# Attention scores of a hybrid decoder layer: from separate bias and maximum passes to one fused VectorE operation per head

## The chip, the cores and the metric

The kernel runs on one core of a Trainium2 chip. The metric is the device time of one execution in microseconds (us). The engines are named as in the profile: PE is TensorE (matmuls; PEld its weight loads), DVE is VectorE, ACT is ScalarE, POOL is GpSimd, SP is SyncE, which mostly issues transfers.

## What is computed

One decoder layer on 512 tokens of width 1024. A modulated norm and one projection feed two causal attention branches; their outputs are projected, gated, summed and normed; then comes a mixture of 32 experts, each token going to 4. Only the scores of the two branches are touched. A: 8 heads of width 64, a window of 128, one learned sink per head. B: 4 heads with two maps each, full causal. Both add a bias that depends on the distance alone, from one table with 32 buckets.

```python
# A (per head): qb holds q / 8
sc = where(valid, qb @ kb.T + bias, -inf)
m = maximum(max(sc, -1), sink)
p = exp(sc - m) / (sum(exp(sc - m)) + exp(sink - m))
# B (per head and map m): distances of 128 and more share one bucket
sc = where(dist >= 0, qb[m] @ k[m].T + bias, -inf)
p[m] = softmax(sc);   a = p[0] - lambda * p[1]
```

## The kernel before

Every engine has its own program, and semaphores tie them together. The stages follow one another: conditioning and norm, the input projection (w_in is streamed in halves, split into high and low parts), attention, the merge (output projection, norms, router, dispatch) and the experts, whose weights are streamed through SBUF.

In the attention stage the work is cut into 24 units: for each of four tiles of 128 queries (n = 0 to 3), two A units (one per group g, four heads in one unit) and four B units (one per head, two maps in one unit). An A unit has 4 rows of scores of 256 keys per query (128 in tile 0). A B unit has 2 rows of (n + 1) x 128 keys; the last 256 of them are "near" and get the table of biases, those before them are "far" and get one value per head.

A unit goes through the engines so. PE makes the scores in PSUM (`scores`, line 401; two pairs of banks in turn). VectorE (`before`, line 486) scales them by QK_SCALE = 1/8, adds the bias and writes them to SBUF: line 496 for an A unit, line 510 for the near part of a B unit, line 514 for the far part (tiles 2 and 3 only); each of these counts up `s_ready`. Then it reduces the maximum of each row (line 499 or 517) and negates it (line 501, with the sink, and line 504 for A; line 519 for B). ScalarE takes the exponentials with their sums (line 593). VectorE (`after`, line 521) divides (lines 529 to 533) or combines the two maps (lines 536 to 541). PE transposes the result (lines 430, 434), ScalarE copies that to SBUF (line 609), PE multiplies by the values (lines 451, 459). At the end of a tile a norm runs over B's outputs: squares on ScalarE (line 621), `sub_norm_begun` and `sub_norm` on VectorE (line 557 writes `on`), a power on POOL, four transposes on PE (line 467).

The order of the work is written out by hand: each engine walks over the units in a loop, VectorE with `after(i + 1)`, then `before(i + 3)`; ScalarE with the copy of i, the exponentials of i + 2, the outputs of i - 1; PE with the scores of i + 3, the transposes of i, the values of i - 1. PE's scores of unit i wait until the scores of unit i - 2 have been read out of PSUM (`s_ready`, line 405). The values of the first B unit of a tile wait for the norm of the tile before (line 457). Between VectorE's units 2 and 3 stand three operations (lines 565 to 569); line 565 needs `grow3`, whose load POOL issues behind the last columns of the input projection.

The bias tables are made long before: a matmul of the bucket table with a one-hot matrix gives vectors of 384 biases by distance, VectorE copies them to `rv` (line 1785), POOL stores them to HBM and reads them back shifted by one per partition as `toep` (128 queries x 12 heads x 256 keys). `farb` is the bias of the last bucket, and `sinkb` the sinks, for each partition. Masked places hold -1e30.

Of the kernel before, what the change touches and what calls it, by code (L numbers as in the profile page):

```python
# [14 lines left out]
F32 = mybir.dt.float32  # L15
# [8 lines left out]
P = 128  # L24
# [6 lines left out]
H_B = 4  # L31
# [65 lines left out]
def program(nc, ctx, x, c, rel_bias_table, w_ada, b_ada, g_mix_pre, g_mix_post, g_ffn_pre, g_ffn_post, w_in, w_out,  # L97
# [122 lines left out]
    nhalf = small("nhalf", [P, H_B], F32)  # L220
    cact = small("cact", [P, KC], F32)
    sinkb = small("sinkb", [P, H_A], F32)
    nsink = small("nsink", [P, H_A], F32)
    farb = small("farb", [P, H_B], F32)
    subg = small("subg", [P, 1], F32)
    subgs = small("subgs", [P, 1], F32)
    nlam0 = small("nlam0", [P, 1], F32)
# [13 lines left out]
    lprod = at("lprod", [P, 2, DH], F32, 158 * KB)  # L241

    st = at("st", [P, IN_FLIGHT, 8, 4], F32, 35 * KB)
    NMX, MX, DSK, ESK, SUM, DEN, FAC = range(7)
    sn = at("sn", [P, 3, H_B], F32, 35 * KB + 512)
    bsum = at("bsum", [P, 2, H_B], F32, 35 * KB + 576)
    beps = at("beps", [P, H_B], F32, 35 * KB + 608)
# [40 lines left out]
    def sem(name):  # L288
# [19 lines left out]
    s_ps, s_ready, mx_step, exp_ready, den_step, p_ready, t_ps, pt_ready, o_ps, o_ready = map(  # L308
        sem, ("s_ps", "s_ready", "mx_step", "exp_ready", "den_step", "p_ready", "t_ps", "pt_ready", "o_ps",
              "o_ready"))  # L310
    osq_ready, sn_ready, on_ready, ot_ps, ot_ready = map(
        sem, ("osq_ready", "sn_ready", "on_ready", "ot_ps", "ot_ready"))

# [45 lines left out]
    def total(count, i):  # L359
        return sum(count(u) for u in UNITS[:i + 1])  # L360

    def n_scores(u):
        return 2 if u[0] == "B" and u[1] >= 2 else 1

    def n_max(u):
        return 3 if u[0] == "A" else 2

    def n_exp(u):
        return 5 if u[0] == "A" else 2
# [30 lines left out]
    def attention_pe(pe):  # L400
        def scores(i):
            kind, n, g = UNITS[i]
            w = 2 * (i % 2)
            if i >= 2:
                pe.wait_ge(s_ready, total(n_scores, i - 2))
            if kind == "A":
                k0, k1 = keys(UNITS[i])
                for place in range(4):
                    a, b = place // 2, place % 2
                    lo = (place % 2) * 2 * P + (P if n == 0 else 0)  # L410
                    ins = nc.tensor.matmul(ps[:, w + a, lo:lo + (k1 - k0) * P],
                                           qk[64 * a:64 * a + 64, 2 * g + b, n * P:(n + 1) * P],
                                           ka2[64 * a:64 * a + 64, g, k0 * P:k1 * P], start=True, stop=True)
            else:
                for m in range(2):
                    ins = nc.tensor.matmul(ps[:, w + m, 0:(n + 1) * P], qk[64 * m:64 * m + 64, 4 + g, n * P:(n + 1) * P],
                                           qk[64 * m:64 * m + 64, 8 + g, 0:(n + 1) * P], start=True, stop=True)
            ins.then_inc(s_ps, 1)
# [64 lines left out]
    def attention_dve(dve):  # L483
        dve.wait_ge(toep_in, 16 * 5)

        def before(i):
# [6 lines left out]
            src, dst = scores_ps(i), scores_sb(i)  # L493
            if kind == "A":
                lo = P if n == 0 else 0
                nc.vector.scalar_tensor_tensor(dst, src, QK_SCALE, toep[:, 4 * g:4 * g + 4, lo:2 * P], ALU.mult,
                                               ALU.add).then_inc(s_ready, 1)
                dve.wait_ge(s_ready, total(n_scores, i))
                nc.vector.tensor_reduce(st[:, w, MX, :], dst, AX_X, ALU.max).then_inc(mx_step, 1)
                dve.wait_ge(mx_step, total(n_max, i) - 2)  # L500
                nc.vector.scalar_tensor_tensor(st[:, w, NMX, :], st[:, w, MX, :], -1.0, nsink[:, 4 * g:4 * g + 4],
                                               ALU.mult, ALU.min).then_inc(mx_step, 1)
                dve.wait_ge(mx_step, total(n_max, i) - 1)
                nc.vector.tensor_tensor(st[:, w, DSK, :], st[:, w, NMX, :], sinkb[:, 4 * g:4 * g + 4],
                                        ALU.add).then_inc(mx_step, 1)
                return
            near = max(n - 1, 0) * P
            width = (n + 1) * P - near
            tile = toep[:, H_A + g:H_A + g + 1, 2 * P - width:2 * P].to_broadcast([P, 2, width])
            nc.vector.scalar_tensor_tensor(dst[:, :, near:near + width], src[:, :, near:near + width], QK_SCALE, tile,  # L510
                                           ALU.mult, ALU.add).then_inc(s_ready, 1)
            if near:

                nc.vector.tensor_scalar(dst[:, :, 0:near], src[:, :, 0:near], QK_SCALE, farb[:, g:g + 1], ALU.mult,
                                        ALU.add).then_inc(s_ready, 1)
            dve.wait_ge(s_ready, total(n_scores, i))
            nc.vector.tensor_reduce(st[:, w, MX, 0:2], dst, AX_X, ALU.max).then_inc(mx_step, 1)  # L517
            dve.wait_ge(mx_step, total(n_max, i) - 1)
            nc.vector.tensor_scalar(st[:, w, NMX, 0:2], st[:, w, MX, 0:2], -1.0, None, ALU.mult).then_inc(mx_step, 1)

        def after(i):
# [1175 lines left out]
    def _(dve):  # L1697
# [84 lines left out]
        for b in range(2):  # L1782
            n = (H_A, H_B)[b]
            dve.wait_ge(rv_ps, b + 1)
            nc.vector.tensor_copy(rv[0:n, b, :], ps[0:n, 6 + b, 0:REL]).then_inc(rv_ready, 1)
        dve.wait_ge(small_in, 16 * N_SMALL)
        nc.vector.tensor_tensor(lprod[:], lp[:, 0::2, :], lp[:, 1::2, :], ALU.mult).then_inc(lam_step, 1)
        dve.wait_ge(lam_step, 1)
        nc.vector.tensor_reduce(lsum[:], lprod[:], AX_X, ALU.add).then_inc(lam_step, 1)
        nc.vector.tensor_scalar(subgs[:], subg[:], 1.0 - LAM_INIT, None, ALU.mult).then_inc(lam_step, 1)  # L1790
        nc.vector.tensor_scalar(nsink[:], sinkb[:], -1.0, None, ALU.mult).then_inc(lam_step, 1)
        dve.wait_ge(bada_in, 16)

        def unit(u, last=False):
# [130 lines left out]
```

## Time and profile before

| | us |
|---|---|
| median of 3 runs | 1743.36 (1741.38 to 1743.51) |
| profiled execution | 1744.51 |
| its span | 1742.2 |
| granted TensorE clock, mean over the span | 0.964 |
| attention stage, VectorE's first to last operation | 244.25 to 334.18 |
| first matmul of the merge that is on the chain of waits | 335.34 |

The profile comes from one execution. Times of instructions are counted from the start of the span; "busy" is the time in which an engine executes an instruction. The granted clock is a share of TensorE's full 2.4 GHz, so that 0.5 is 1.2 GHz. Two instructions of one engine can overlap in the timeline, since one starts while its forerunner writes out its last results.

### The profile page before, as it was taken

Reading aid. Unit: us, or ns where it says so; the run is one execution under the profiler, and the core shown is the slowest. Engines: PE = TensorE matmul, PEld = TensorE weight load, DVE = VectorE, ACT = ScalarE, POOL = GpSimd, SP = SyncE. Lnnn points to the kernel's source line nnn. Section 1 sums busy time; section 2 is a strip of 40 time slices with the busy share of each in tenths; the row PEclk is TensorE's granted clock in tenths of the full one; section 3 lists DMA queues with packets and bytes.
Section 4 is the critical chain, followed back from the end, with each engine's and each line's share of the span. In section 5 each row is a group of like instructions: output and inputs, shape, how many; then the busy total and the mean of one; then the engine's idle time right before and its main releaser. Section 6 shows DMA issues by size and latency. Waiting matters only on the chain.

```text
span 1742.2 us, 19602 instructions
## 1 busy us (share of the span) xinstructions
PE 1650.7 (95%) x7482; PEld 1294.0 (74%) x7482; DVE 1372.9 (79%) x1017; ACT 1098.0 (63%) x903; POOL 200.1 (11%) x156
## 2 busy tenths in 40 slices
PE   8999988787699999999999999999999999999994
PEld 3888865443478888888888888888888888888882
DVE  5564459545589898889988898989888998889894
ACT  3323236612467777777777777777777777777772
POOL 2200000202200100011000100010001100021112
PEclk9999998897699999999999999999999999999997
DMA  9865530113699999999999999999999999999964
GB/s 340 249 236 193 169 118 1 52 73 105 245 406 399 375 368 387 390 380 354 387 380 384 359 375 389 389 383 366 379 378 390 358 390 389 380 357 371 383 238 158
DMA packets 156725, 540.93 MB, mean 310 GB/s; under 512 B 13980, under 2 KB 15112, under 8 KB 156515
## 3 DMA queue, kind: packets, MB, share of 16 engines
q1 hardware_dynamic: 140880, 500.20, 75.5%
q0 software_dynamic: 13648, 35.26, 8.4%
q10 hardware_dynamic: 2100, 4.21, 0.7%
q8 instruction: 57, 0.93, 0.2%
q14 instruction: 40, 0.33, 0.0%
HBM read 522.94 MB, written 29.66 MB: 317 GB/s over the span
## 4 chain that ended last, share of the span: by engine, by line
PE 80%; issue 8%; DVE 5%; DMA 4%; ACT 1%; POOL 1%; POOLq 0%; SPq 0%; ACTq 0%; DVEq 0%
PE ps L1113 65%; PE ps L661 4%; PE ps L1087 4%; PE ps L1103 2%; PE ps L1622 1%; PE ps L1624 1%; PE ps L1623 1%; DMA raw<-in_w_ada 1%; DMA oh<-const_buckets 1%; PE ps L681 1%; DMA grow<-in_g_ffn_post 0%; DVE st L517 0%; DMA expert_sums<-yb,icur 0%; DMA xb<-h_ffn,stab 0%; DVE acc L1721 0%
## 5 line engine op out<-in xcount | busy, mean ns | idle before, releaser
L1231 DVE TENSOR_TENSOR wl<-rawm,wh 128x2048 fp32r<-128x2048 f32 x420 | 946.7, 2286 | 147.7 <-ACT wh L1160 143.2
L1160 ACT ACTIVATE wh<-rawm 128x2048 fp32r<-128x2048 f32 x420 | 802.0, 1919 | 260.8 <-PE ps L1113 260.8
L1113 PE MATMUL ps<-wh,xh 128*128 128x512 f32 x1120 | 360.3, 403 | 3.5 <-DVE xl L1244 3.5
L1113 PE MATMUL ps<-wl,xh 128*128 128x512 f32 x1120 | 346.8, 391 | 0.0
L1113 PE MATMUL ps<-wh,xl 128*128 128x512 f32 x1120 | 346.3, 390 | 0.0
L1113 PEld LDWEIGHTS ps<-wh,xh 128*128 128x128 f32 x1120 | 211.3, 189 | 53.2 <-DVE xl L1244 4.9
L1113 PEld LDWEIGHTS ps<-wl,xh 128*128 128x128 f32 x1120 | 211.1, 189 | 44.9
L1113 PEld LDWEIGHTS ps<-wh,xl 128*128 128x128 f32 x1120 | 211.4, 189 | 44.5
L1113 PE MATMUL ps<-wh,ah 128*128 128x512 f32 x560 | 179.4, 401 | 2.5 <-DVE al L1248 2.5
L1113 PE MATMUL ps<-wl,ah 128*128 128x512 f32 x560 | 174.1, 392 | 0.0
L1113 PE MATMUL ps<-wh,al 128*128 128x512 f32 x560 | 173.1, 390 | 0.0
L1316 POOL DMA_INDIRECT expert_sums<-yb,stab x32 | 50.9, 1589 | 1009.0 <-ACT yb L1194 752.1
L1113 PEld LDWEIGHTS ps<-wh,al 128*128 128x128 f32 x560 | 105.6, 189 | 23.1
L1113 PEld LDWEIGHTS ps<-wl,ah 128*128 128x128 f32 x560 | 105.4, 188 | 22.7
L1113 PEld LDWEIGHTS ps<-wh,ah 128*128 128x128 f32 x560 | 100.3, 189 | 19.6 <-issue 3.0
L1758 DVE TENSOR_TENSOR wlf<-raw,whf 128x2048 fp32r<-128x2048 f32 (+1 forms) x18 | 39.1, 2173 | 70.1 <-ACT whf L1483 70.1
L1483 ACT ACTIVATE whf<-raw 128x2048 fp32r<-128x2048 f32 (+1 forms) x18 | 32.7, 1818 | 67.7 <-PE ps L1624 61.3
L1622 PE MATMUL ps<-whf,hh 128*128 128x512 f32 (+1 forms) x192 | 71.3, 372 | 0.0
L1305 POOL DMA_INDIRECT xb<-h_ffn,stab x32 | 65.7, 2053 | 47.7 <-PE ps L1087 36.2
L1624 PE MATMUL ps<-whf,hl 128*128 128x512 f32 (+1 forms) x192 | 71.0, 370 | 0.0
L1623 PE MATMUL ps<-wlf,hh 128*128 128x512 f32 (+1 forms) x192 | 71.0, 370 | 0.0
L1186 ACT ACTIVATE ah<-ps 128x1024 fp32r<-128x1024 f32 x35 | 35.9, 1026 | 55.3 <-PE ps L1113 55.3
(256 smaller groups left out, 1588.2 us busy)
## 6 DMA issues: line engine op xcount, KB each, us to landing
rawm<-in_w_gate_up SPq DMA_DIRECT2D x280, 1024.0 KB, 9.8
rawm<-in_w_down SPq DMA_DIRECT2D x140, 1024.0 KB, 7.9
raw<-in_w_ada SPq DMA_DIRECT2D x20, 1024.0 KB, 5.9
raw<-in_w_in SPq DMA_DIRECT2D x16, 1024.0 KB, 5.6
rawx<-in_w_ada SPq DMA_DIRECT2D x4, 1024.0 KB, 15.7
wo<-in_w_out SPq DMA_DIRECT2D x2, 2048.0 KB, 12.6
bias_vectors_repeated<-bias_vectors POOLq DMA_DIRECT2D x1, 2304.0 KB, 15.2
xs<-in_x ACTq DMA_DIRECT2D x1, 2048.0 KB, 12.8
```

Source lines behind the costliest of these rows:

```text
L661: ins = nc.tensor.matmul(ps[:, 2 * b + half, :], src[:, k, t * P:(t + 1) * P], wo[:, 4 * b + k, half * UN:(half + 1) * UN], start=(k == 0) ...
L1087: ins = nc.tensor.transpose(TURNED[:, k // 4, (k % 4) * P:(k % 4 + 1) * P], src[:, k * P:(k + 1) * P], ident[:])
L1113: ins = nc.tensor.matmul(banks[:, n, :], left[:, kk, :], right[:, k, n * UN:(n + 1) * UN], start=begins and kk == 0 and i == 0, stop=kk == ...
L1160: nc.scalar.activation(flat(wh[v % SPL][:]), flat(rawm[v][:]), ACT.Copy).then_inc(wh_done, 1)
L1186: nc.scalar.activation(flat(ah[:]), flat(TURNED), ACT.Copy).then_inc(ah_done, 1)
L1231: nc.vector.tensor_tensor(flat(wl[v][:]), flat(rawm[v][:]), flat(wh[v % SPL][:]), ALU.subtract).then_inc(wl_done, 1)
L1305: pool.indirect_dma_start(out=xb[:], out_offset=None, in_=h2_d, in_offset=bass.IndirectOffsetOnAxis(ap=column(0, p, gcur, p - (E - 1)), ax ...
L1316: pool.indirect_dma_start(out=sum_d, out_offset=bass.IndirectOffsetOnAxis(ap=column(1, p, done, p - (E - 1) if done is scur else 1), axis= ...
L1622: nc.tensor.matmul(dst, a_h, b_h, start=first, stop=False)
L1623: nc.tensor.matmul(dst, a_h, b_l, start=False, stop=False)
L1624: return nc.tensor.matmul(dst, a_l, b_h, start=False, stop=last)
L1758: nc.vector.tensor_tensor(wlf[:, m_slot, :, 0:n], raw[:, slot, :, 0:n], whf[:, m_slot, :, 0:n], ALU.subtract).then_inc(raw_used, 1)
```

## The change

It takes one row of scores per partition, so an A unit needs four of them and a B unit one per map and part. Since the scale now comes after the addition, the tables hold the biases times 8: the copy into `rv` becomes a multiplication, and `farbs` is `farb` times 8. The sink is the start value in A units, so the operation that held the negated sinks (`nsink`) goes. In tiles 2 and 3 the far part of a map runs first and its maximum (`FMX`) is the start value of the near part, which waits for it (`far_step`). `s_ready` now counts one per unit, after the last fused operation.

```diff
-                nc.vector.scalar_tensor_tensor(dst, src, QK_SCALE, toep[:, 4 * g:4 * g + 4, lo:2 * P], ALU.mult,
-                                               ALU.add).then_inc(s_ready, 1)
-                dve.wait_ge(s_ready, total(n_scores, i))
-                nc.vector.tensor_reduce(st[:, w, MX, :], dst, AX_X, ALU.max).then_inc(mx_step, 1)
-                dve.wait_ge(mx_step, total(n_max, i) - 2)
-                nc.vector.scalar_tensor_tensor(st[:, w, NMX, :], st[:, w, MX, :], -1.0, nsink[:, 4 * g:4 * g + 4],
-                                               ALU.mult, ALU.min).then_inc(mx_step, 1)
+                for h in range(4):
+                    ins = nc.vector.tensor_tensor_reduce(dst[:, h, :], src[:, h, :], toep[:, 4 * g + h, lo:2 * P], QK_SCALE,
+                                                         sinkb[:, 4 * g + h:4 * g + h + 1], ALU.add, ALU.max,
+                                                         st[:, w, MX, h:h + 1])
+                ins.then_inc(s_ready, 1)
+                dve.wait_ge(s_ready, i + 1)
+                nc.vector.tensor_scalar(st[:, w, NMX, :], st[:, w, MX, :], -1.0, None, ALU.mult).then_inc(mx_step, 1)
...
-            nc.vector.scalar_tensor_tensor(dst[:, :, near:near + width], src[:, :, near:near + width], QK_SCALE, tile,
-                                           ALU.mult, ALU.add).then_inc(s_ready, 1)
             if near:
-
-                nc.vector.tensor_scalar(dst[:, :, 0:near], src[:, :, 0:near], QK_SCALE, farb[:, g:g + 1], ALU.mult,
-                                        ALU.add).then_inc(s_ready, 1)
-            dve.wait_ge(s_ready, total(n_scores, i))
-            nc.vector.tensor_reduce(st[:, w, MX, 0:2], dst, AX_X, ALU.max).then_inc(mx_step, 1)
-            dve.wait_ge(mx_step, total(n_max, i) - 1)
+                for m in range(2):
+                    nc.vector.tensor_tensor_reduce(dst[:, m, 0:near], src[:, m, 0:near],
+                                                   farbs[:, g:g + 1].to_broadcast([P, near]), QK_SCALE, LOWEST, ALU.add,
+                                                   ALU.max, st[:, w, FMX, m:m + 1]).then_inc(far_step, 1)
+            for m in range(2):
+                if near:
+                    dve.wait_ge(far_step, total(n_far, i) - 1 + m)
+                ins = nc.vector.tensor_tensor_reduce(dst[:, m, near:near + width], src[:, m, near:near + width],
+                                                     toep[:, H_A + g, 2 * P - width:2 * P], QK_SCALE,
+                                                     st[:, w, FMX, m:m + 1] if near else LOWEST, ALU.add, ALU.max,
+                                                     st[:, w, MX, m:m + 1])
+            ins.then_inc(s_ready, 1)
+            dve.wait_ge(s_ready, i + 1)
...
-            nc.vector.tensor_copy(rv[0:n, b, :], ps[0:n, 6 + b, 0:REL]).then_inc(rv_ready, 1)
+            nc.vector.tensor_scalar(rv[0:n, b, :], ps[0:n, 6 + b, 0:REL], 1.0 / QK_SCALE, None, ALU.mult).then_inc(rv_ready, 1)
...
-        nc.vector.tensor_scalar(nsink[:], sinkb[:], -1.0, None, ALU.mult).then_inc(lam_step, 1)
+        nc.vector.tensor_scalar(farbs[:], farb[:], 1.0 / QK_SCALE, None, ALU.mult).then_inc(lam_step, 1)
```

## Rows read from the trace of the kernel before

**Rows 1.** The page: busy time, share of the span and instructions of each engine.
```profile
PE 1650.7 (95%) x7482; PEld 1294.0 (74%) x7482; DVE 1372.9 (79%) x1017; ACT 1098.0 (63%) x903; POOL 200.1 (11%) x156
```
**Rows 2.** Busy time by stretch: length, engines, then granted clock, DMA share, GB/s.
```profile
250.00:323.00 73.00, 55.56 (x360) 38.86 (x360) 68.64 (x154) 49.85 (x171) 3.58 (x4) 0.87 0.08 29
264.00:270.00 6.00, 3.97 (x17) 3.10 (x18) 5.69 (x14) 4.09 (x15) 0.00 (x0) 0.60 0.00 0
323.00:335.00 12.00, 7.79 (x48) 7.47 (x49) 3.04 (x10) 4.28 (x15) 2.56 (x4) 0.79 0.25 89
```
**Rows 3.** The chain of waits, from 225 to 360 us: start, length, what.
```profile
240.33 8.34 DMA grow<-in_g_ffn_post
...
248.70 1.23 DVE gpf L565
...
335.34 24.84 PE ps L661 x52
```
**Rows 4.** VectorE's timeline: start, length, operation, out and in.
```profile
252.11 0.42 DVE L510 SCALAR_TENSOR_TENSOR s_sb<-ps,toep 128x256 f32<-128x256 f32 x1
...
253.02 0.17 DVE L519 TENSOR_SCALAR st<-st 128x2 f32<-128x2 f32 x1
...
258.07 1.22 DVE L496 SCALAR_TENSOR_TENSOR s_sb<-ps,toep 128x1024 f32<-128x1024 f32 x1
...
260.58 0.16 DVE L501 SCALAR_TENSOR_TENSOR st<-st,nsink 128x4 f32<-128x4 f32 x1
...
265.89 0.68 DVE L510 SCALAR_TENSOR_TENSOR s_sb<-ps,toep 128x512 f32<-128x512 f32 x1
...
267.33 0.17 DVE L519 TENSOR_SCALAR st<-st 128x2 f32<-128x2 f32 x1
...
285.32 0.68 DVE L510 SCALAR_TENSOR_TENSOR s_sb<-ps,toep 128x512 f32<-128x512 f32 x1
...
287.41 0.17 DVE L519 TENSOR_SCALAR st<-st 128x2 f32<-128x2 f32 x1
...
307.47 0.68 DVE L510 SCALAR_TENSOR_TENSOR s_sb<-ps,toep 128x512 f32<-128x512 f32 x1
308.07 0.74 DVE L514 TENSOR_SCALAR s_sb<-ps,farb 128x512 f32<-128x512 f32 x1
...
310.10 0.17 DVE L519 TENSOR_SCALAR st<-st 128x2 f32<-128x2 f32 x1
310.17 0.15 DVE L529 TENSOR_TENSOR st<-st 128x4 f32<-128x4 f32 x1
310.36 0.18 DVE L531 RECIPROCAL st<-st 128x4 f32<-128x4 f32 x1
```
**Rows 5.** VectorE's groups, shapes apart: count, busy us, mean ns, idle before.
```profile
L510 DVE SCALAR_TENSOR_TENSOR s_sb<-ps,toep 128x512 f32<-128x512 f32 x12 | 8.2, 682 | 0.0
...
L541 DVE SCALAR_TENSOR_TENSOR s_sb<-s_sb,st 128x256 f32<-128x256 f32 x4 | 1.9, 484 | 0.1
L514 DVE TENSOR_SCALAR s_sb<-ps,farb 128x256 f32<-128x256 f32 x4 | 1.9, 474 | 0.0
...
L510 DVE SCALAR_TENSOR_TENSOR s_sb<-ps,toep 128x256 f32<-128x256 f32 x4 | 1.7, 416 | 0.0
...
L541 DVE SCALAR_TENSOR_TENSOR s_sb<-s_sb,st 128x128 f32<-128x128 f32 x4 | 1.4, 352 | 0.1
```
**Rows 6.** ScalarE's timeline: a sum's readout, and the next exponential.
```profile
261.88 0.19 ACT L593 ACTIVATION_READ_ACCUMULATOR s_sb<-s_sb,st 128x1 f32 x1
261.97 0.49 ACT L593 ACTIVATE s_sb<-s_sb,st 128x256 f32<-128x256 f32 x1
```
**Rows 7.** PE's, ScalarE's and VectorE's timelines in tile 1; brackets: idle before, releaser.
```profile
266.03 1.97 PE L430 MATMUL ps<-ident,s_sb 128*128 128x128 f32 x8 [2.49 <-DVE s_sb L533]
...
268.08 1.02 ACT L609 ACTIVATE pt<-ps 128x1024 f32<-128x1024 f32 x1 [1.45 <-issue]
...
273.55 0.16 DVE L536 RECIPROCAL st<-st 128x1 f32<-128x1 f32 x1 [0.37 <-ACT s_sb L593]
```

More of the change, by code:

```diff
@@ L222, in program @@
     sinkb = small("sinkb", [P, H_A], F32)
-    nsink = small("nsink", [P, H_A], F32)
     farb = small("farb", [P, H_B], F32)
+    farbs = small("farbs", [P, H_B], F32)
     subg = small("subg", [P, 1], F32)
@@ L243, in program @@
     st = at("st", [P, IN_FLIGHT, 8, 4], F32, 35 * KB)
-    NMX, MX, DSK, ESK, SUM, DEN, FAC = range(7)
+    NMX, MX, DSK, ESK, SUM, DEN, FAC, FMX = range(8)
+    LOWEST = -3e38
     sn = at("sn", [P, 3, H_B], F32, 35 * KB + 512)
@@ L310, in program @@
               "o_ready"))
+    far_step = sem("far_step")
     osq_ready, sn_ready, on_ready, ot_ps, ot_ready = map(
@@ L360, in total, with n_far @@
         return sum(count(u) for u in UNITS[:i + 1])
-    def n_scores(u):
-        return 2 if u[0] == "B" and u[1] >= 2 else 1
+    def n_far(u):
+        return 2 if u[0] == "B" and u[1] >= 2 else 0
     def n_max(u):
-        return 3 if u[0] == "A" else 2
+        return 2 if u[0] == "A" else 1
     def n_exp(u):
@@ L404, in scores @@
             if i >= 2:
-                pe.wait_ge(s_ready, total(n_scores, i - 2))
+                pe.wait_ge(s_ready, i - 1)
             if kind == "A":
@@ L508, in before @@
             width = (n + 1) * P - near
-            tile = toep[:, H_A + g:H_A + g + 1, 2 * P - width:2 * P].to_broadcast([P, 2, width])
-            nc.vector.scalar_tensor_tensor(dst[:, :, near:near + width], src[:, :, near:near + width], QK_SCALE, tile,
-                                           ALU.mult, ALU.add).then_inc(s_ready, 1)
             if near:
-                nc.vector.tensor_scalar(dst[:, :, 0:near], src[:, :, 0:near], QK_SCALE, farb[:, g:g + 1], ALU.mult,
-                                        ALU.add).then_inc(s_ready, 1)
-            dve.wait_ge(s_ready, total(n_scores, i))
-            nc.vector.tensor_reduce(st[:, w, MX, 0:2], dst, AX_X, ALU.max).then_inc(mx_step, 1)
-            dve.wait_ge(mx_step, total(n_max, i) - 1)
+                for m in range(2):
[11 more added lines that the diff above has]
+            dve.wait_ge(s_ready, i + 1)
             nc.vector.tensor_scalar(st[:, w, NMX, 0:2], st[:, w, MX, 0:2], -1.0, None, ALU.mult).then_inc(mx_step, 1)
```

## The prediction

> **What bounds the kernel now.** I read first the page's busy times: TensorE (PE) is busy for 95% of the span and VectorE (DVE) for 79% [rows 1], so by the average a VectorE edit should bring nothing. The change lies in the attention stage alone, so I asked for busy times by stretch. In the stretch from 250 to 323 us VectorE is busy 68.64 of 73 us, PE 55.56 at a mean granted clock of 0.87, ScalarE (ACT) 49.85; from 323 to 335 us VectorE is busy for only 3.04 of 12, a tail that belongs to PE and ACT [rows 2]. So the engine that the change relieves is the bound of this stage, and nearly without gaps. The chain of waits says how the stage is fixed at its ends: VectorE's first units are followed by a load of the last norm weights that lands at 248.68, and the merge's matmuls follow the last transposes at 335.34 [rows 3]. PE then goes from the merge without a pause longer than a few us into the experts, whose loads are released by work of the merge. I find nothing between 335 us and the end that holds to a time of its own, so what the attention stage loses or gains should arrive at the end of the kernel whole.
>
> **What is removed and added, per unit.** Units 0 to 2 come ahead of line 565, which starts at 248.70, 0.02 us after that load has landed [rows 3]. Whatever they save is waited away there: they count as nothing, and the cover is that load; if it landed earlier they would bring some 0.2 us each. There are 21 units left: 3 B units of tile 0, and in each of tiles 1, 2 and 3 two A and four B. What goes is the bias pass, the far pass and the reduction. From the start of the first of them to the start of the negated maximum, VectorE's timeline gives [rows 4]: an A unit 260.58 - 258.07 = 2.51 us; a B unit of tile 0 253.02 - 252.11 = 0.91, of tile 1 267.33 - 265.89 = 1.44, of tile 2 287.41 - 285.32 = 2.09, of tile 3 310.10 - 307.47 = 2.63.
>
> What comes is four fused operations in an A unit, two in a B unit of tiles 0 and 1, four in one of tiles 2 and 3: 6 + 24 + 8 + 16 + 16 = 70 in the 21 units. No row of before is such an operation, so its price is put together. Streaming: line 510 at 256 columns takes 416 ns from PSUM with a table beside it, and at 512 columns 682, so 128 columns are 133 ns and the fixed part about 150. Where an operand is a per-partition scalar in memory the fixed part is larger: line 541 takes 484 at 256 columns, line 514 takes 474 [rows 5]. The fused operation starts its maximum from such a scalar in A units (the sink) and in the near part of tiles 2 and 3 (the far maximum), from a constant elsewhere. Overlap: line 514 starts at 308.07 where line 510 started at 307.47 and ran for 0.68, so an operation that waits for nothing starts 0.08 before its forerunner ends [rows 4]. Writing out the maximum: the nearest rows are ScalarE's, where each exponential with a sum is followed by a read of the accumulator that delays the next one by 261.97 - 261.88 = 0.09 us [rows 6]; I take that. The last of a unit is waited for, which gives back the 0.08 and adds 0.03, 0.11 in all.
>
> The Trainium skill says the like for VectorE ("VectorE: DVE Perf Modes", the section on two Vector instructions with no wait between them): an op that writes out its accumulator is two instructions, the main one and a read. No row of before shows it on this engine.
>
> So a step costs, from start to start: 256 columns with a constant 0.416 - 0.08 + 0.09 = 0.426; 256 with a scalar 0.484 - 0.08 + 0.09 = 0.494; 128 with a constant 0.293. Per unit:
> - A: 4 x 0.494 + 0.11 = 2.09, saves 0.42; six of them, 2.52.
> - B, tile 0: 2 x 0.293 + 0.11 = 0.70, saves 0.21; three, 0.63.
> - B, tile 1: 2 x 0.426 + 0.11 = 0.96, saves 0.48; four, 1.92.
> - B, tile 2: 2 x 0.293 + 2 x 0.494 + 0.11 = 1.68, saves 0.41; four, 1.64.
> - B, tile 3: 2 x 0.426 + 2 x 0.494 + 0.11 = 1.95, saves 0.68; four, 2.72.
>
> VectorE's own saving is 9.4 us. The negated maximum and its neighbour keep their count and shape. The near operations wait for the far maximum of the same map; the far operation of the other map, 0.29 us or more, lies between, so I cost those waits at nothing (bound: 0.03 us each, 16 of them, 0.5 us). In the prologue a copy becomes a multiplication of the same shape and one small scaling takes the place of another, far from any limit: nothing.
>
> **What is given back.** Three places where VectorE is not alone on the path.
> - Tile 0's B units: VectorE already waits for ScalarE in them, and they run on latency; I count their 0.63 as lost.
> - Tile 1: VectorE's A unit ends shortly before 266.03, PE transposes it for 1.97 us (stretch at a granted clock of 0.60, after 2.49 us of idling), ScalarE copies it at 268.08 and works through exponentials, squares and the next copy, and VectorE waits 0.37 us for it at 273.55 [rows 2, 7]. That chain has no part that the change shortens, so the 3 x 0.48 = 1.44 us of the three B units inside it are lost.
> - The head of tile 3: by the same pattern PE starts late (after the norm of tile 1) and slow; one A unit's 0.42 is lost.
>
> That leaves 9.4 - 0.63 - 1.44 - 0.42 = 6.9, say 7 us. A later release goes against it too: PE may overwrite a score bank once it is read. In an A unit that was the end of the first pass, 1.22 us after its start; it becomes the end of the fourth operation, about 2.0. The unit starts some 0.4 earlier by then, and PE has up to 2.49 us of idle time behind it [rows 7], so I cost it at nothing; without that cover it would be 0.4 us for each of six. For it: shorter idling of PE may keep its clock up. I leave that out of the sum and in the range.
>
> **Size.** The profiled execution took 1744.51 us (span 1742.2); the median of the three runs is 1743.36. 1744.51 - 7 = 1737.5 against its own time; against the median 1736.4.
>
> **Rivals.**
> (1) More than that, 10 to 13 us. The maximum comes out with no extra time and a scalar start costs no more than a constant: 70 x 0.09 + 40 x 0.068 = 9 us on top of 9.4 for VectorE. It could not all arrive: PE's 55.56 and ScalarE's 49.85 us in the same 73 [rows 2] have dependences of their own. I cap it at 13: 1730 to 1733. For it: the engine streams one column per cycle in all rows. Against it: ScalarE's rows.
> (2) About nothing, 1 to 3 us. The read of the maximum waits for its main operation, as a dependent small operation does. Of two small operations line 531 depends on line 529 and starts 310.36 - 310.17 = 0.19 us after it, while line 529, which depends on nothing before it, starts 0.07 after line 519 [rows 4]; 0.10 more on 70 operations is 7.0 us and leaves 2.4: 1741.
> (3) Slower. VectorE takes two cycles per column when it has two streams to read and a running maximum to keep. 56 operations of 256 columns at 0.267 and 14 of 128 at 0.133 add 16.8 us; less 9.4, that is 7.4 more: 1750.8. The point from which it decides is 9.4 / 70 = 0.135 us extra for each operation. Against it: line 541 has two streams, both in SBUF, and takes 484 - 352 = 132 ns for 128 columns, one per cycle [rows 5]; but it keeps no maximum. The Trainium skill has a rule that speaks for it ("Vector Engine (DVE) Microarchitecture Reference", points that are easy to get wrong): a two-source operation with two SBUF sources that aren't bf16 halves its throughput, as both read ports are taken. Here one source is in PSUM. Line 541 does not show the halving.
> (4) The edit does what it says, but another engine sets the pace at once, and under 3.5 us arrive. ScalarE and PE would have to be full, and the rows by stretch say that they aren't.
>
> **Chances.** The forecast (3.5 to 10 us gained) 0.57, rival 1 0.15, rival 2 0.12, rival 3 0.09, rival 4 0.07. About 0.2%, 3.5 us, is what a measurement of this kernel can tell from no change. So faster 0.72, same 0.19, slower 0.09. The range leaves out rival 3 and the outer parts of 1 and 2: 1731 to 1741.5.
>
> **What would show it.** Right: fused rows at about 0.42 us for 256 columns with a short read behind each; A units of 2.1 us where they were 2.51; VectorE still the busiest engine, its busy time in the stage down by about 9 us; line 565 still starting where the weight load lands; a wait for ScalarE at the end of tile 1 longer than 0.37 us; the merge starting near 328.5 us in place of 335.34, and everything behind it in the same distance. Wrong: fused rows of 0.7 us (rival 3); rows 0.19 us apart from their reads (rival 2); VectorE idle behind PE in tiles 2 and 3 (rival 4); or a merge that starts earlier while the end of the span doesn't move.

## The result and the profile after

The changed kernel ran at a median of 1731.36 us (1726.85 to 1733.94, 6 runs) beside 1743.42 (1741.35 to 1747.59, 6 runs) for the kernel before on the same chip. The ratio is 0.9922 [0.9907, 0.9937], a gain of 13.6 us (11.0 to 16.2). The forecast was 7.0 us and a time of 1736.4; 0.9922 x 1743.36 is 1729.8, just under the range's lower end of 1731. The sign was right, the size came out at nearly twice the forecast.

The page of the kernel after, busy time of each engine; VectorE was at 1372.9 us before [rows 1]:

```profile
PE 1640.2 (95%) x7482; PEld 1286.4 (75%) x7482; DVE 1358.4 (79%) x1121; ACT 1096.8 (64%) x903; POOL 200.5 (12%) x156
```

Its chain of waits, in order of time (start, length, what):

```profile
240.04 8.29 DMA grow<-in_g_ffn_post
248.35 1.23 DVE gpf L571
...
319.79 25.30 PE ps L667 x55
```

Line 571 is line 565 of before. It still starts when its load lands, 248.35 us for 248.70, so the first three units gave nothing, as counted. The merge starts at 319.79 where it stood at 335.34 [rows 3]. The stage between these two points is 71.44 us long, it was 86.64. From the merge's first matmul to the end of the span it is 1742.2 - 335.34 = 1406.9 us before and 1724.8 - 319.79 = 1405.0 after (1403.3 to 1407.3 in the 14 profiles of this document), so what the stage gains arrives at the end whole, as the prediction had it.

VectorE's timeline of the kernel after (start, length, operation, out and in; brackets: idle before, releaser):

```profile
251.77 0.28 DVE L519 CUSTOM_DVE_ANT_0 s_sb<-ps,toep 128x128 f32<-128x128 f32 x1
...
252.31 0.17 DVE L525 TENSOR_SCALAR st<-st 128x2 f32<-128x2 f32 x1
...
253.44 0.16 DVE L542 RECIPROCAL st<-st 128x1 f32<-128x1 f32 x1 [0.96 <-ACT s_sb L599]
...
257.59 0.48 DVE L499 CUSTOM_DVE_ANT_0 s_sb<-ps,toep,sinkb 128x256 f32<-128x256 f32 x1
258.00 0.08 DVE L499 DVE_READ_ACCUMULATOR2_ANT st<- 128x1 f32 x1
258.00 0.48 DVE L499 CUSTOM_DVE_ANT_0 s_sb<-ps,toep,sinkb 128x256 f32<-128x256 f32 x1
...
259.33 0.17 DVE L504 TENSOR_SCALAR st<-st 128x4 f32<-128x4 f32 x1
...
263.90 0.42 DVE L519 CUSTOM_DVE_ANT_0 s_sb<-ps,toep 128x256 f32<-128x256 f32 x1
...
264.70 0.17 DVE L525 TENSOR_SCALAR st<-st 128x2 f32<-128x2 f32 x1
...
270.59 0.17 DVE L542 RECIPROCAL st<-st 128x1 f32<-128x1 f32 x1 [1.25 <-ACT s_sb L599]
...
280.40 0.28 DVE L513 CUSTOM_DVE_ANT_0 s_sb<-ps,farbs 128x128 f32<-128x128 f32 x1
...
281.74 0.17 DVE L525 TENSOR_SCALAR st<-st 128x2 f32<-128x2 f32 x1
...
298.09 0.42 DVE L513 CUSTOM_DVE_ANT_0 s_sb<-ps,farbs 128x256 f32<-128x256 f32 x1
...
299.70 0.17 DVE L525 TENSOR_SCALAR st<-st 128x2 f32<-128x2 f32 x1
```

The second fused operation of an A unit starts at 258.00, at the same moment as the read of the first one's maximum and 0.08 us before the first one ends (257.59 + 0.48 = 258.07). The read has a row of its own and delays nothing. From the first operation of a unit to its negated maximum it is now 259.33 - 257.59 = 1.74 us for an A unit (2.51 before [rows 4]), and for a B unit of tiles 0 to 3 0.54, 0.80, 1.34 and 1.61 us (0.91, 1.44, 2.09, 2.63).

VectorE's groups of the fused operation and of its read, shapes apart (count, busy us, mean ns, idle before):

```profile
L499 DVE CUSTOM_DVE_ANT_0 s_sb<-ps,toep,sinkb 128x256 f32<-128x256 f32 x24 | 10.2, 479 | 0.1
...
L519 DVE CUSTOM_DVE_ANT_0 s_sb<-ps,toep,st 128x256 f32<-128x256 f32 x16 | 7.1, 479 | 0.0
...
L519 DVE CUSTOM_DVE_ANT_0 s_sb<-ps,toep 128x256 f32<-128x256 f32 x8 | 3.0, 419 | 0.0
...
L519 DVE DVE_READ_ACCUMULATOR2_ANT st<- 128x1 f32 x32 | 2.7, 83 | 0.0
...
L499 DVE CUSTOM_DVE_ANT_0 s_sb<-ps,toep,sinkb 128x128 f32<-128x128 f32 x8 | 2.3, 346 | 1.3 <-PE ps L413 1.3
...
L519 DVE CUSTOM_DVE_ANT_0 s_sb<-ps,toep 128x128 f32<-128x128 f32 x8 | 2.1, 284 | 0.1
```

A constant start costs 419 ns at 256 columns, a scalar start 479, and 128 columns more are 479 - 346 = 133 ns, the price that line 541 had in before, 484 - 352 = 132 [rows 5]. The idle time ahead of them is nearly nothing, but for 1.3 us once in tile 0, ahead of the last norm weights. So PE fed VectorE in time in this execution.

The stretches of the kernel after, with the columns of rows 2:

```profile
250.00:257.00 7.00, 5.98 (x39) 4.25 (x41) 5.30 (x28) 4.30 (x17) 0.39 (x1) 0.66 0.73 274
257.00:262.00 5.00, 3.64 (x25) 2.12 (x23) 4.77 (x23) 3.58 (x16) 0.00 (x0) 1.00 0.00 0
262.00:309.00 47.00, 39.85 (x298) 28.09 (x298) 43.66 (x193) 40.36 (x138) 3.06 (x3) 1.00 0.00 1
```

VectorE is still the busiest engine of tiles 1 to 3, with 43.66 of 47 us. PE's granted clock is 1.00 (2.4 GHz) there, and 0.89 in the same part of before. These are the two stretches of before that answer to tiles 1 to 3 and to what follows them:

```profile
262.00:323.00 61.00, 46.28 (x301) 32.55 (x299) 58.06 (x122) 43.19 (x145) 3.06 (x3) 0.89 0.00 1
323.00:327.00 4.00, 3.83 (x20) 3.86 (x21) 2.19 (x8) 0.98 (x4) 0.00 (x0) 0.57 0.00 0
```

The second one is in the stage's **tail**, from the value products that wait for the norm of tile 2 to the merge, where VectorE is no longer the bound. I call what lies ahead of it, from line 565/571 on, the **body**. PE's rows at the border, of before:

```profile
323.18 2.02 PE L459 MATMUL ps<-nat,pt 128*128 128x128 f32 x8 [2.75 <-DVE on L557]
```

and of after:

```profile
264.03 1.09 PE L432 MATMUL ps<-ident,s_sb 128*128 128x128 f32 x8 [1.24 <-DVE s_sb L539]
...
309.74 1.13 PE L461 MATMUL ps<-nat,pt 128*128 128x128 f32 x8 [1.58 <-DVE on L563]
```

The body went from 323.18 - 248.70 = 74.48 to 309.74 - 248.35 = 61.39 us, the tail from 12.16 to 10.05.

### The profile page after: what moved, and what is told of

Read it like the earlier page. It is cut to its first block, busy times and chain, and to the rows that moved or that the text cites. A ratio compares the mean times of both kernels' runs of the same rounds, so it can differ in the third digit from the quotient of the medians.

```text
span 1724.8 us, 19706 instructions
## 1 busy us (share of the span) xinstructions
PE 1640.2 (95%) x7482; PEld 1286.4 (75%) x7482; DVE 1358.4 (79%) x1121; ACT 1096.8 (64%) x903; POOL 200.5 (12%) x156
## 4 chain that ended last, share of the span: by engine, by line
PE 82%; issue 8%; DVE 5%; DMA 3%; ACT 1%; POOL 0%; POOLq 0%; SPq 0%; ACTq 0%; DVEq 0%
PE ps L1119 66%; PE ps L1093 4%; PE ps L667 4%; PE ps L1109 2%; PE ps L1628 1%; PE ps L1629 1%; PE ps L1630 1%; DMA raw<-in_w_ada 1%; PE ps L687 1%; DMA grow<-in_g_ffn_post 0%; DMA expert_sums<-yb,icur 0%; DMA xb<-h_ffn,stab 0%; DVE acc L1727 0%; DVE s_sb L519 0%; DVE s_sb L499 0%
```

## The experiments

Each kernel's total is its ratio to the kernel before on the same chip; body, tail and stage come from its one profiled execution, in us.

| kernel | ratio [95%] | body | tail | stage |
|---|---|---|---|---|
| before | 1 | 74.48 | 12.16 | 86.64 |
| before again | 0.9998 [0.9987, 1.0008] | 75.60 | 12.38 | 87.98 |
| after | 0.9922 [0.9907, 0.9937] | 61.39 | 10.05 | 71.44 |
| after, second time | 0.9920 [0.9907, 0.9934] | 63.70 | 10.51 | 74.21 |
| after, third time | 0.9922 [0.9907, 0.9937] | 63.65 | 10.51 | 74.16 |
| A units alone | 0.9982 [0.9973, 0.9991] | 73.88 | 12.37 | 86.25 |
| B units alone | 0.9939 [0.9924, 0.9955] | 67.30 | 10.05 | 77.35 |
| constant start in A | 0.9917 [0.9903, 0.9930] | 60.66 | 10.06 | 70.72 |
| small operation behind each | 0.9927 [0.9913, 0.9940] | 67.34 | 10.51 | 77.85 |
| delay ahead of the norm of tile 2 | 0.9937 [0.9922, 0.9952] | 62.33 | 10.51 | 72.84 |
| delay in tile 3 | 0.9913 [0.9898, 0.9929] | 62.44 | 10.51 | 72.95 |
| constant start, first unit early | 0.9902 [0.9887, 0.9918] | 60.55 | 10.05 | 70.60 |
| before, PE kept busy | 0.9973 [0.9961, 0.9985] | 74.99 | 10.02 | 85.01 |
| best: early, PE kept busy | 0.9882 [0.9869, 0.9896] | 59.25 | 9.99 | 69.24 |

**The kernels themselves, repeated.** The first, second and last of these runs have no edit.

> The changed kernel once more, to see what of its 12 us (medians 1743.42 and 1731.36) and of the 17 us between the two profiled executions holds. Theory T (VectorE's own saving, 15.4 us by the rows of after, arrives nearly whole because PE's clock no longer falls in the attention stage, which gives some 2 us more in the tail and pays for about 1 to 2 us of new waits for ScalarE): the merge's first matmul starts within 1 us of 319.8, PE is granted 1.00 from 262 to 313 us, ratio 0.990 to 0.993; what differs between executions lies behind the attention stage. Rival R (the attention stage itself varies by several us from execution to execution, and the profiled one was lucky): the merge starts at 323 or later and the clock falls to 0.5 somewhere between 262 and 313 us.

> The kernel before once more, for a second profile. The executions so far show the fall of PE's clock at different places, so the one profile of before may be a poor or a good one. Theory T: from the start of the last norm weights' multiplication to the merge's first matmul 85 to 88 us (86.64 in the first profile), with the clock at 0.5 in two to four stretches; ratio 0.999 to 1.001. If it takes 84 or less, part of the gain between the two profiled executions was chance.

> The changed kernel a third time, beside the kernel before with and without the added transposes. Theory T: stage 71 to 74.5 us, the longer ones with a slow PE in tile 0; ratio 0.9910 to 0.9935, a gain of 11.5 to 15.5 us, of which VectorE's own saving is 15.4 at most.

The totals repeat: three ratios of 0.992 for after, and 0.9998 for before against itself. The single profiled executions don't: the first one of after was 2.7 us shorter in the stage than the other two. The third one's stretches show where:

```profile
250.00:257.00 7.00, 5.75 (x31) 4.04 (x33) 5.31 (x28) 3.58 (x15) 0.52 (x1) 0.50 0.73 280
257.00:262.00 5.00, 4.80 (x31) 2.98 (x28) 3.33 (x17) 2.70 (x13) 0.00 (x0) 0.83 0.01 3
262.00:312.00 50.00, 41.78 (x301) 29.64 (x301) 45.83 (x200) 42.46 (x147) 3.06 (x3) 0.97 0.00 1
```

In tile 0 the granted clock is 0.50, then 0.83, where the first execution had 0.66 and 1.00. PE's scores come late, and VectorE waits for them at the head of tile 1; in tile 1 it waits twice for ScalarE, 0.83 and 1.25 us, where the first execution had the 1.25 alone (its timeline in this execution):

```profile
259.31 0.48 DVE L499 CUSTOM_DVE_ANT_0 s_sb<-ps,toep,sinkb 128x256 f32<-128x256 f32 x1 [1.02 <-PE ps L413]
...
269.83 0.16 DVE L542 RECIPROCAL st<-st 128x1 f32<-128x1 f32 x1 [0.83 <-ACT s_sb L599]
...
273.17 0.16 DVE L542 RECIPROCAL st<-st 128x1 f32<-128x1 f32 x1 [1.25 <-ACT s_sb L599]
```

The second execution has the same waits, 1.06 us at 260.93 and then 0.83 and 1.25. The wait at the head of tile 1 isn't of the change's making: the second execution of before has it too, with the old operations (its VectorE timeline):

```profile
259.29 1.23 DVE L496 SCALAR_TENSOR_TENSOR s_sb<-ps,toep 128x1024 f32<-128x1024 f32 x1 [1.30 <-PE ps L411]
```

So the gain of the body is best taken from means: (74.48 + 75.60) / 2 = 75.04 less (61.39 + 63.70 + 63.65) / 3 = 62.91 makes 12.1 us; the tail, 12.27 less 10.36, makes 1.9. Together 14.0, and the ratio says 13.6.

**A units alone.** In the B units the old operations come back, and their table its old scale:

```diff
-                for m in range(2):
-                    nc.vector.tensor_tensor_reduce(dst[:, m, 0:near], src[:, m, 0:near],
...
+                ins = nc.vector.tensor_scalar(dst[:, :, 0:near], src[:, :, 0:near], QK_SCALE, farb[:, g:g + 1], ALU.mult,
+                                              ALU.add)
...
+            nc.vector.tensor_reduce(st[:, w, MX, 0:2], dst, AX_X, ALU.max).then_inc(mx_step, 1)
```

> Only the A units are fused; the B units keep bias pass, far pass and reduction, with tables that are not scaled. VectorE saves 6 x 0.77 = 4.6 us in units 3 to 23. Theory T: a gain of 4 to 5 us, plus at most 2 where PE's idle stretches (1.98 to 2.75 us in the kernel before) become short enough for the clock to hold; the merge starts at 329 to 331. Rival (what is saved on VectorE is lost to PE or ScalarE if it is small): under 3 us, merge at 333 or later.

The six A units save 6 x 0.77 = 4.6 us of VectorE's time, but the body is only 75.04 - 73.88 = 1.2 shorter. VectorE's timeline of this kernel shows what took it back:

```profile
259.19 0.48 DVE L499 CUSTOM_DVE_ANT_0 s_sb<-ps,toep,sinkb 128x256 f32<-128x256 f32 x1 [1.04 <-PE ps L413]
...
301.54 0.48 DVE L499 CUSTOM_DVE_ANT_0 s_sb<-ps,toep,sinkb 128x256 f32<-128x256 f32 x1 [0.83 <-PE ps L413]
...
304.87 0.16 DVE L533 TENSOR_TENSOR st<-st 128x4 f32<-128x4 f32 x1 [1.22 <-ACT st L600]
```

At the heads of tiles 1 and 3 a slow PE is behind (granted clock 0.50 from 250 to 257 us, 0.81 from 290 to 300), and once ScalarE. The first of these waits is the one that before again has as well. The second place is the loss at the head of tile 3 that the prediction had, and here it is 0.83 us. The total gains 3.1 us (0.9982; 1.6 to 4.7), more than the 1.1 us of the stage; it can't be told from the 4 to 5 that were expected.

**B units alone.** The A units are as before, with `nsink` and three steps:

```diff
-                for h in range(4):
-                    ins = nc.vector.tensor_tensor_reduce(dst[:, h, :], src[:, h, :], toep[:, 4 * g + h, lo:2 * P], QK_SCALE,
...
+                nc.vector.scalar_tensor_tensor(dst, src, QK_SCALE, toep[:, 4 * g:4 * g + 4, lo:2 * P], ALU.mult,
+                                               ALU.add).then_inc(s_ready, 1)
...
+                nc.vector.tensor_reduce(st[:, w, MX, :], dst, AX_X, ALU.max).then_inc(mx_step, 1)
```

> Only the B units are fused; the A units keep bias pass, reduction and the negated maximum with the sink. VectorE saves 3 x 0.37 + 4 x 0.64 + 4 x 0.75 + 4 x 1.02 = 10.8 us. Theory T: less the 1.1 us of tile 0 and up to 1.5 in tile 1, 8 to 10 us, and 2 more if the clock holds in the tail; the merge starts at 324 to 327. If the parts add up, this gain and that of the kernel with fused A units alone make the whole one; if the clock counts, they make less, since each alone leaves some idle stretch of PE at 2 us or more.

The body gains 7.7 us of the 10.8 that the B units save VectorE, the tail 2.2, the total 10.6 (0.9939). The two halves sum to 3.1 + 10.6 = 13.7, the whole is 13.6. In the totals the parts add up, to within some 4 us. In the single profiled executions they do so less well: the stage gains 1.1 with the A units, 10.0 with the B units and 14.0 with both. The tail's gain comes with the B units alone (10.05, and 12.37 with the A units).

**Constant start in A units.** The sink goes from the start of the maximum to the negated maximum:

```diff
-                                                         sinkb[:, 4 * g + h:4 * g + h + 1], ALU.add, ALU.max,
+                                                         LOWEST, ALU.add, ALU.max,
...
-                nc.vector.tensor_scalar(st[:, w, NMX, :], st[:, w, MX, :], -1.0, None, ALU.mult).then_inc(mx_step, 1)
+                nc.vector.scalar_tensor_tensor(st[:, w, NMX, :], st[:, w, MX, :], -1.0, nsink[:, 4 * g:4 * g + 4],
+                                               ALU.mult, ALU.min).then_inc(mx_step, 1)
```

> As the changed kernel, but the fused operations of the A units start from a constant, and the sink comes in with the negated maximum, as in the kernel before. By the rows of after a 256-column fused operation takes 479 ns with a scalar start and 418 with a constant: 24 of them in the A units of tiles 1 to 3, 24 x 0.06 = 1.5 us less on VectorE. Theory T: the A units' rows fall to 0.42 us, an A unit to 1.50 us from start to start of the negated maximum, and the merge starts 1.0 to 1.5 us earlier than in the changed kernel (near 318.5); in total time 0 to 2 us faster, hardly to be told by the median. Rival (ScalarE has become the bound): the rows shrink and the merge's start moves by less than 0.4 us.

Its group of A operations:

```profile
L500 DVE CUSTOM_DVE_ANT_0 s_sb<-ps,toep 128x256 f32<-128x256 f32 x24 | 8.7, 419 | 0.1
```

479 ns became 419: the scalar start costs 60 ns. The prediction's 68 ns from other operations' rows held. The stage is 70.72 us, 0.7 under the shortest of after, so half of the 24 x 0.06 = 1.4 us arrives: VectorE now waits 0.60 us for ScalarE at 278.42, where it didn't before. The totals (0.9917, 0.9922) can't be told apart.

**A small operation behind each fused one.** It stands in for a readout that would cost time:

```diff
+                    ins = nc.vector.tensor_scalar(pad[:, h:h + 1], one[:], 1.0, None, ALU.mult)
...
+                    nc.vector.tensor_scalar(pad[:, m:m + 1], one[:], 1.0, None, ALU.mult)
...
+                ins = nc.vector.tensor_scalar(pad[:, 2 + m:3 + m], one[:], 1.0, None, ALU.mult)
```

> The changed kernel with one tiny VectorE operation (128x1) behind each fused one, where the prediction had put the readout of the maximum: by the rows so far a free operation of that size delays the next by about 0.08 us, so VectorE gets 70 x 0.08 = 5.6 us more in units 3 to 23. Theory S (the prediction's main error is that it priced the readout at 0.09 us each, 6.3 us, where it costs the next operation nothing): rows of 0.48 us follow one another at 0.48 to 0.50 us in place of 0.404; from the start of the last norm weights' multiplication to the merge's first matmul it takes 75.5 to 77.5 us in place of 71.4, and the total gain falls from 13 to about 8 us. Rival (another engine paces the stage by now, VectorE's time is slack): under 2 us of it show, less than 73.5 us and a gain of 11 or more.

VectorE's timeline of this kernel, at its first A unit of tile 1:

```profile
263.52 0.48 DVE L500 CUSTOM_DVE_ANT_0 s_sb<-ps,toep,sinkb 128x256 f32<-128x256 f32 x1 [1.33 <-PE ps L414]
263.93 0.08 DVE L500 DVE_READ_ACCUMULATOR2_ANT st<- 128x1 f32 x1
263.93 0.15 DVE L503 TENSOR_SCALAR pad<-one 128x1 f32<-128x1 f32 x1
264.00 0.47 DVE L500 CUSTOM_DVE_ANT_0 s_sb<-ps,toep,sinkb 128x256 f32<-128x256 f32 x1
```

Now it is the small operation that starts together with the read, and the fused one behind it starts 264.00 - 263.52 = 0.48 us after its forerunner, 0.07 later than without. From here to the tail's start at 319.89 it is 56.37 us; from the same unit to the same place it was 309.74 - 257.59 = 52.15 in the first execution of after and 53.00 in the second and the third. 64 operations of 0.067 are 4.3 us, and 3.4 to 4.2 of them show. So in this execution most of a delay of 0.07 us on each fused operation reaches the tail, and a readout of 0.09 would have cost most of what the prediction charged. The totals don't confirm it. The gain was expected to fall to about 8 us, and by the ratio it is 12.7 (10.5 to 15.2), which is 0.9 under that of after, with 3 to 4 either way; at 1739.61 us the profiled execution was the slowest of this kernel's five. How much of the delay reaches the end stays open.

**A delay ahead of the norm of tile 2, and one elsewhere.** A memset of 0.86 us of VectorE's time on a free buffer makes PE's wait ahead of the tail longer; the control has it in the middle of tile 3.

```diff
+                if tile_ended(i - 3) == 2:
+                    nc.vector.memset(h2s[:, 1, 0:960], 0.0)
```

```diff
+                if i == 18:
+                    nc.vector.memset(h2s[:, 1, 0:960], 0.0)
```

> The changed kernel with a memset of 960 columns (about 1.05 us) on VectorE just ahead of the norm of tile 2, for whose result PE waits 1.58 us. PE's idling there becomes about 2.6 us, as long as in the kernel before (2.75). Theory C (PE's clock falls behind an idle stretch of some 2 us and more, and the slow matmuls behind it lengthen the tail): the granted clock falls to 0.5 behind that wait, the first value products take 2.0 us in place of 1.13, and the merge starts 2.5 to 3.5 us later than in the changed kernel. Rival (the tail was shorter for another reason, or by chance): clock 1.00 and the merge 1.0 us later.

> The control to the delay in the tail: the same memset on VectorE in the middle of tile 3, between the division of the second A unit and the scores of the second last group, where PE has work of its own. Theory C: PE's longest idling there stays under 1.6 us, the clock stays at 1.00 and the merge starts 0.9 to 1.2 us later than in the changed kernel. If it costs 2 us or more with the clock at 1.00, VectorE's place in the tail decides and not the clock.

This tried theory C, that PE's last wait ahead of the tail, by its length of over 2 us, makes the tail slow. PE's timeline of the first kernel at that wait:

```profile
312.38 1.13 PE L461 MATMUL ps<-nat,pt 128*128 128x128 f32 x8 [2.52 <-DVE on L563]
```

The wait is 2.52 us, near the 2.75 of before, and the eight products take 1.13, not 2.02. Theory C falls, and not because 2.52 is a little less than 2.75: in tile 2 the two executions of before have the same transposes behind the same wait, slow in the first and fast in the second (PE's timelines):

```profile
285.46 1.81 PE L430 MATMUL ps<-ident,s_sb 128*128 128x128 f32 x8 [2.27 <-DVE s_sb L533]
```

```profile
286.24 1.09 PE L430 MATMUL ps<-ident,s_sb 128*128 128x128 f32 x8 [2.28 <-DVE s_sb L533]
```

From the other side, PE's timeline of the third execution of after and of the control:

```profile
265.75 1.97 PE L432 MATMUL ps<-ident,s_sb 128*128 128x128 f32 x8 [1.24 <-DVE s_sb L539]
```

```profile
264.60 1.19 PE L432 MATMUL ps<-ident,s_sb 128*128 128x128 f32 x8 [1.25 <-DVE s_sb L539]
```

A wait of 1.24 us stands ahead of transposes at the lower level in the one, and one of 1.25 ahead of fast ones in the other, as in the first execution of after. The length of the last idle stretch doesn't decide alone. The tail is 10.51 in both, as in the second and third execution of after. The 0.46 over the first one's 10.05 is the last four transposes: they took 1.11 or 1.12 us here and 0.66 there, behind a wait of 3.8 us in each. The bodies, 62.33 and 62.44, are 0.9 and 1.1 us longer than the first execution's 61.39, whose waits they share; so a delay of 0.86 us on VectorE reaches the tail. The totals (0.9937, 0.9913) have intervals that overlap.

**First unit ahead of the norm weights.** With the constant start:

```diff
+        after(0)
         dve.wait_ge(grow_in, 48)
...
-        after(0)
```

> The constant start of the A units, and the division of unit 0 moved ahead of the multiplication by the last norm weights, for whose load VectorE now waits 0.66 to 1.26 us. PE's first transposes start some 1.5 us earlier, its idle stretch ahead of them falls from 3.7 or 4.3 to 2.5 to 3 us. Theory T: the stage from that load's landing to the merge shortens by 0.7 to 1.2 us against the constant start alone (70.7 us), since unit 0's division no longer stands behind it; the clock still falls at the stage's head. Rival (tile 0 runs on ScalarE's and PE's latency and gives it all back): less than 0.3 us.

The stage is 70.60 us, 0.1 under the constant start alone. The head of tile 1 gives back what the move brought; VectorE's timeline of this kernel:

```profile
257.26 0.42 DVE L500 CUSTOM_DVE_ANT_0 s_sb<-ps,toep 128x256 f32<-128x256 f32 x1 [1.33 <-PE ps L414]
```

The rival of this experiment held. The total, 0.9902, is the lowest so far, and its interval overlaps that of 0.9917.

**Before, with PE kept busy.** The old VectorE code; PE transposes the identity into a free bank in places where it would wait:

```diff
-            pe.wait_ge(p_ready, i + 1)
...
+            for _ in range(16 if i == 0 else 12 if kind == "A" and n and g == 0 else 0):
+                nc.tensor.transpose(ps[:, 4, 0:P], ident[:], ident[:])
+            pe.wait_ge(p_ready, i + 1)
...
+                    for _ in range(10 if n > 1 else 0):
+                        nc.tensor.transpose(ps[:, 5, 0:P], ident[:], ident[:])
```

> The kernel before, with idle PE given transposes of the identity into PSUM that nobody reads: 16 ahead of the first transposes, 12 ahead of those of each tile's first A unit, 10 ahead of the value products that wait for a norm (tiles 2 and 3). They run while PE would wait. It is the clock alone, with no change on VectorE. Theory C2 (the clock's fall costs the kernel before about 2 us, in the tail, and little elsewhere since VectorE is the bound): the stage takes 84 to 85.5 us in place of 86.64 and the clock stays at 1.00 in more of it; ratio 0.9985 to 0.9995. Rival (the clock has no part in the gain): 86 us or more. If it falls to 82, the clock is worth more than the tail.

Its stretches, and in the second fence PE's timeline at the border of the tail:

```profile
262.00:325.00 63.00, 49.07 (x368) 35.24 (x365) 60.26 (x128) 44.75 (x151) 3.06 (x3) 1.00 0.00 1
325.00:335.00 10.00, 5.64 (x46) 5.27 (x47) 3.37 (x10) 4.62 (x15) 2.00 (x3) 1.00 0.29 106
```

```profile
325.42 1.16 PE L463 MATMUL ps<-nat,pt 128*128 128x128 f32 x8 [1.51 <-DVE on L561]
```

The clock is 1.00 through tiles 1 to 3, yet the body is 74.99 us, the mean of before being 75.04: with the old operations VectorE sets the body, and a faster PE brings next to nothing there. In tile 0 the clock still fell (0.60 from 257 to 262 us), and VectorE waits 1.30 us at the head of tile 1, as in before again. Beside that execution's 75.60 the body is 0.6 shorter, about the 0.60 us wait for ScalarE in tile 0, which is gone. The tail is 10.02 in place of 12.27. That tells the two sources apart: the body's gain is VectorE's, the tail's is the clock's. The total gains 4.7 us (2.6 to 6.8), more than the tail's 2.3 and than the 0.9 to 2.6 us that were expected; where the rest is stays open.

**The version that beats both.** Constant start, first unit early, and a few transposes of the identity:

```diff
+            for _ in range(10 if i == 0 else 2 if kind == "A" and n and g == 0 else 0):
+                nc.tensor.transpose(ps[:, 4, 0:P], ident[:], ident[:])
...
+        for _ in range(26):
+            nc.tensor.transpose(ps[:, 5, 0:P], ident[:], ident[:])
```

> The constant start and the early first division, and such transposes of the identity in PE's idle stretches: 10 ahead of the first transposes, 2 ahead of each tile's first A unit, 26 ahead of the last transposes of the stage, where PE waits 3.8 us for the last norm and the merge's first 6 us run at a clock of 0.5 behind it. Theory C: the merge's first matmuls run at full clock, which brings the stretch from the merge's start to the first expert matmul down by 2 us or more from 124.4; the stage stays at 70 to 71 us; total 1725 to 1727, ratio 0.988 to 0.990. Rival (the clock falls whatever PE is given, or the transposes delay real work): no change in the merge, or the last transposes start later by 1 us and more.

1723.97 us at the median, 0.9882 [0.9869, 0.9896], 20.6 us under before and clear of after's interval. The stage is 69.24 us, 18.1 under the mean of the two executions of before. Behind it the merge seems to gain a little too. The chain of waits of this kernel from the merge on, and below it that of the first execution of after:

```profile
317.64 27.47 PE ps L675 x64
```

```profile
319.79 29.16 PE ps L667 x64
```

The chain's first 64 matmuls of the merge take 1.7 us less where PE comes to them from transposes of the identity with a wait of 0.96 us, and not of 3.80. The granted clock of the merge's first 6.4 us is 1.00 in place of 0.73. In the 13 other profiles these 64 take 28.34 to 29.99 us, so 27.47 is the shortest, by 0.9 us; the profile of this kernel is one. Each of the three additions by itself lies within what the totals can tell, the sum of them doesn't.

## Why the prediction failed in size

**What held.** VectorE bounds the body: a full clock alone left it at 74.99 us. The load covers units 0 to 2: line 571 starts where it lands. The waits of the near operations for the far maximum cost nothing: the idle time of that group is 0.0. Streaming, the fixed part, the dearer scalar start (40 operations) and the overlap of 0.08 us were right to within 10 ns each. Rival 3 is out: 128 columns cost 133 ns. The rule in the Trainium skill ("Vector Engine (DVE) Microarchitecture Reference", points that are easy to get wrong) that two SBUF sources that aren't bf16 halve the throughput doesn't reach an operation with one source in PSUM by these rows.

**The step that failed: "Writing out the maximum".** The prediction took the 0.09 us by which ScalarE's reads delay the next exponential [rows 6], since VectorE had no such row. It charged 70 x 0.09 = 6.3 us. Measured, the read takes 83 ns on its row and 0 on the path, for the next operation starts with it. Start to start it is 0.41 us in place of 0.494 for 256 columns with a scalar, 0.34 in place of 0.426 with a constant and 0.21 in place of 0.293 for 128. The units save 6 x 0.77 + 3 x 0.37 + 4 x 0.64 + 4 x 0.75 + 4 x 1.02 = 15.4 us, not 9.4. The Trainium skill says rightly that such an operation is two instructions ("VectorE: DVE Perf Modes", two Vector instructions with no wait between them); that the second one costs time was my addition. Rival 1 named this case with half of its mechanism (free readout, but also a scalar start as cheap as a constant, which was wrong) and gave it 0.15; the measured 13.6 lies just above its cap of 13 us. In the profile of the kernel with a small operation behind each, most of 0.07 us on each reaches the tail, though its totals don't confirm it.

**A term left out: the tail.** "For it: shorter idling of PE may keep its clock up. I leave that out of the sum and in the range." The clock brought 1.9 us, in the tail, where VectorE's pace doesn't matter. Before with PE kept busy shows that it is the clock. That shorter idling is what kept it up is not shown: with the wait at the border made 2.52 us long the clock stayed up too. The rows for a slow tail were there: rows 2 have 0.79 for it, and in the trace of before its first eight value products, at 323.18, run for 2.02 us. I had a slow stretch only as a delay, not as one that could go.

**What was given back: 3.2 us, forecast 2.5.** That is the 15.37 of the units less the body's 12.13, in means. Most of it is time in which VectorE waits for ScalarE ahead of the reciprocals (line 536, now 542) in tiles 0 and 1: 1.0 and 0.6 us in the two executions of before, 2.5, 3.8 and 3.8 in the three of after. That is 2.6 us more, where 0.63 + 1.44 = 2.1 was forecast for the two places. In tile 1 alone the wait went from 0.37 us [rows 7] to 1.25 in the first execution, where PE's transposes were fast (1.09 us), and to 0.83 + 1.25 in the two others, where they took 1.97 as in rows 7. The loss at the head of tile 3 didn't come in any of the three (0.1 us of idle time ahead of 24 A operations in the first), but did with the A units alone. The head of tile 1 cost 1.06 and 1.02 us in two of the three, and 1.30 in one of the two executions of before, so in the means it takes nothing from the gain. The later release of the score bank, costed at nothing, shows as a longer wait of PE ahead of scores, 1.06 us for 0.58 at 262.09; no wait of VectorE in these profiles is tied to it. Some 0.6 us of the 3.2 isn't placed.

So 15.4 - 3.2 + 1.9 = 14.1 by the profiles, where 9.4 - 2.5 = 6.9 was forecast; the totals, which are separate evidence, say 13.6. Of the difference 6.0 is the unit sum, -0.7 what was given back, and 1.9 the tail. Rival 4 is out: VectorE is busy 43.66 of 47 us in tiles 1 to 3. Rival 2 is out: the read's row stands 0 us, not 0.10, from the next start.

## What to carry to other kernels

When a price has no row on its own engine, give the other engine's row as one end and nothing as the other, and choose by whether somebody waits for the result: here the next fused operation didn't need it, and the charge was multiplied by 70. After an engine's saving, look at the stretches in which the engine isn't the bound: PE's granted clock can change there, and that is a term with a sign and a size of its own. Take a gain of a few us from several profiled executions of both kernels or from the ratio, since one execution of after was 2.7 us shorter in the stage than the two others. Before a wait is laid to the change, look for it in a second execution of before: the one of 1 us at the head of tile 1 was there.

## What the hardware showed that was not expected

- VectorE's row for reading the accumulator is 83 ns long and starts together with the next fused operation; a 128x1 operation behind a fused one puts off the next by 0.07 us, the read by nothing.
- The fused operation with a bias stream, a scale and a running maximum takes 419 ns for 256 columns, as the plain bias pass did at 416; a scalar start adds 60 ns.
- PE's clock didn't follow the length of its last wait: full speed after 2.52 us, the lower level after 1.24, and either after 2.27 and 2.28 at the same place of the same kernel. What decides is open. Filling the waits with useless transposes kept it at 1.00 over 63 us and took 2.3 us from the tail of the kernel before.
